# RWKV scan: chunks of 64 tokens for 32, each 64×64 inverse joined from two 32-row blocks

## What the stage computes

```python
def wkv_scan(r, logw, k, v, a, b, s0):
    def step(s, inp):
        r_t, lw_t, k_t, v_t, a_t, b_t = inp
        sa = jnp.einsum('dbhij,dbhj->dbhi', s, a_t)
        s = s * jnp.exp(lw_t)[..., None, :] + sa[..., None] * b_t[..., None, :] + v_t[..., None] * k_t[..., None, :]
        return s, jnp.einsum('dbhij,dbhj->dbhi', s, r_t)
    s_fin, y = lax.scan(step, s0, (tm(r), tm(logw), tm(k), tm(v), tm(a), tm(b)))

def rwkv_readout(y, prep, r_k, lnx_g, lnx_b, w_out):
    yf = y[0] + jnp.flip(y[1], 1)
    mean = jnp.mean(yf, axis=-1, keepdims=True)
    var = jnp.mean(jnp.square(yf - mean), axis=-1, keepdims=True)
    yn = ((yf - mean) * lax.rsqrt(var + GN_EPS)).reshape(B, T, D).astype(gate.dtype) * lnx_g + lnx_b
    bonus = jnp.sum(r[None] * k_dir * r_k, axis=(0, -1))[..., None] * v
    o = (yn + bonus.reshape(B, T, D)) * jax.nn.silu(gate)
    return o @ w_out
```

## Time and profile before

| | |
|---|---|
| median of 3 runs | 2717.05 us (2715.08 to 2720.73) |
| profiled run | 2720.06 us, span 2718.4 us |
| busy share of the span: PE, PEld, DVE, ACT, POOL | 83%, 64%, 36%, 19%, 2% |
| mean granted clock of TensorE, whole span | 0.858 of full speed |
| scan stage, 1640 to 2353 us | 713 us, of them PE busy 573.3, DVE 307.2, ACT 264.7; clock 0.67 |

### The profile page before, as it was taken

The page is one execution under the profiler, slowest core; times in us unless marked ns, Lnnn a source line. Parts: engine busy times, 40 slices in busy tenths (PEclk is TensorE's granted clock), DMA queues, the critical chain, the costliest instruction groups (busy, mean ns, idle before and its releaser), DMA issues. The chain is left out here.

```text
span 2718.4 us, 39159 instructions
## 1 busy us (share of the span) xinstructions
PE 2245.3 (83%) x16630; PEld 1735.0 (64%) x16630; DVE 984.4 (36%) x2209; ACT 518.1 (19%) x920; POOL 58.2 (2%) x85
## 2 busy tenths in 40 slices
PE   1999955798999886899859993688888889779797
PEld 0888854687888775788624442466666777536445
DVE  3224346411440372675161003544544441120253
ACT  1011022401000101100110003444444333010142
POOL 0000000000000300000000000000000000000000
PEclk9999977898999898899979995776667776689889
DMA  7465410424874321775303203111101111312100
GB/s 289 173 230 228 171 64 8 86 93 165 336 280 155 124 78 37 281 302 217 138 16 109 92 31 125 38 39 38 35 15 39 29 25 41 124 66 93 52 10 16
DMA packets 103014, 305.14 MB, mean 112 GB/s; under 512 B 71352, under 2 KB 79800, under 8 KB 85184
## 3 DMA queue, kind: packets, MB, share of 16 engines
q1 hardware_dynamic: 94384, 225.11, 24.3%
q0 software_dynamic: 8464, 77.60, 7.3%
HBM read 286.88 MB, written 15.80 MB: 111 GB/s over the span
## 5 line engine op out<-in xcount | busy, mean ns | idle before, releaser
L263 PE MATMUL bank<-h,ring 128*128 128x256 f32 x2944 | 646.7, 383 | 22.8 <-DVEq L967 15.3
L263 PEld LDWEIGHTS bank<-h,ring 128*128 128x128 f32 x2944 | 566.3, 193 | 104.0 <-DVEq L967 16.0
L263 PE MATMUL bank<-mixed,ring 128*128 128x512 f32 x384 | 165.0, 592 | 1.3 <-DVE mixed L1249 1.3
L877 PE MATMUL bank<-ffn_hidden,ring 128*128 128x256 f32 x704 | 152.4, 379 | 3.3 <-PEq L903 3.3
L877 PEld LDWEIGHTS bank<-ffn_hidden,ring 128*128 128x128 f32 x704 | 133.6, 190 | 22.2 <-issue 4.1
L263 PEld LDWEIGHTS bank<-mixed,ring 128*128 128x128 f32 x384 | 72.9, 190 | 93.5 <-issue 91.4
L156 DVE CUSTOM_DVE_ANT_0 next_w<-next_w,next_vec,par 128x1024 f32<-128x1024 f32 x96 | 120.1, 1279 | 11.4 <-DMA next_w<-in_mod_stream 11.4
L1987 DVE TENSOR_TENSOR rw_u<-bank,rw_lam 128x128 f32<-128x128 f32 x120 | 35.0, 291 | 236.1 <-PE bank L1660 233.1
L889 DVE SCALAR_TENSOR_TENSOR x<-bank,mod,x 128x256 f32<-128x256 f32 x24 | 10.0, 477 | 231.6 <-PE bank L877 231.6
L1668 PE MATMUL bank<-rw_gr,rw_u 64*64 64x32 f32 x960 | 80.3, 252 | 13.0 <-DVE rw_u L1987 12.9
L1581 PE MATMUL bank<-rw_xa,ring 64*64 64x64 f32 x1024 | 30.5, 305 | 72.2 <-DVE rw_xa L1920 72.2
(11 more groups left out here) (387 smaller groups left out, 3415.1 us busy)
## 6 DMA issues: line engine op xcount, KB each, us to landing
ring<-in_stream SPq DMA_DIRECT2D x89, 2048.0 KB, 8.0
next_w<-in_mod_stream POOLq DMA_DIRECT2D x24, 2048.0 KB, 9.9
ctx<-in_mod_rest POOLq DMA_DIRECT2D x16, 1024.0 KB, 7.3
rwkv_projections<-proj_out POOLq DMA_DIRECT2D x8, 1024.0 KB, 6.7
y<-bias_table SPq DMA_DIRECT2D x48, 128.0 KB, 4.9
rw_rkv<-rwkv_projections SPq DMA_DIRECT2D x8, 768.0 KB, 4.2
rw_at<-rw_at_kept SPq DMA_DIRECT2D x16, 256.0 KB, 3.9
rwkv_o<-rwkv_projections POOLq DMA_DIRECT2D x1, 2048.0 KB, 16.0
```

Source lines behind the costliest of these rows:

```text
L263: mm = pe.matmul(out, ring_tile(k, n, kt, i * P), rhs[kt], start=start and kt == kts[0], stop=stop and kt == kts[-1])
L877: mm = pe.matmul(k.psum[grp * 4 + i][:, 0:T], ring_tile(k, n, kt, i * P), rhs[part * KT + kt], start=(part == 0 and kt == 0), stop=(part = ...
```

## The change

It works in chunks of 64 tokens: 8 chunks, chain items 0 to 8, seven state updates. The inverse stays at 32×32 blocks (`SUB`), 64 of them per n as before: each chunk's 64×64 matrix has two diagonal blocks that VectorE inverts, and the block between them comes from two new products on TensorE, `left` and `join`, each with a ScalarE copy behind it (four items for each n, 16 matmuls of 32×32 with 32 columns each). For `left`, the first diagonal block's inverse is needed transposed too: VectorE copies all inverses in turned order (L1995), SyncE stores part of that in four more DMAs (L1537, 64-byte runs) and loads it in two more (L1544). SyncE also waits for `left` of the n before (`left_up`) ahead of the loads.

Keys of a chunk lie on rows 0 to 63 and second factors on rows 64 to 127. So akv and pq use one 64×64 tile, `inner` and `read_inner` tiles of 128 rows by 64 columns, `carried` and `read_state` 64×64; grams fill 64×128 and come in four halves for each n, masked in pieces of 256 elements. The gate is loaded for each n. The two numbers that place an item list in the period change for five lists.

```diff
-LCH = 32
+LCH = 64
+SUB = 32
 NCK = 512 // LCH
...
 def scan_solve(n):
 
+    out = [("left", n, 0), ("atok", n, 0, 0), ("left", n, 1), ("atok", n, 0, 1), ("join", n, 0)]
+    for d in range(2):
+        out += [("akv", n, d, e) for e in range(2)]
+        out += [("atok", n, 1, half) for half in range(2)] + [("join", n, 1)] if d == 0 else []
+        out += [("pq", n, d, e, half) for half in range(2) for e in range(2)]
+        out += [("gr", n, d)]
+    return out
...
-                            (0, 0.7, has(i + 1, scan_solve(i + 1))),
-                            (0, 0.3, has(i + 2, scan_grams(i + 2))),
+                            (0, 0.75, has(i + 1, scan_solve(i + 1))),
+                            (0.1, 0.42, has(i + 2, scan_grams(i + 2))),
                             (0, 0.3, has(i - 1, scan_read(i - 1))),
...
-                            (0.45, 1, has(i + 2, [("inv", i + 2, s) for s in range(1, LCH)])),
-                            (0.42, 1, has(i + 3, scan_ready(i + 3))))
+                            (0.55, 1, has(i + 2, [("inv", i + 2, s) for s in range(1, SUB)])),
+                            (0.48, 0.9, has(i + 3, scan_ready(i + 3))))
...
                 for q in range(2):
                     sp.dma_start(own_rows(mt_dram, n, q), Xb[rows64(q)]).then_inc(x_out, 16)
-                sp.wait_ge(x_out, 32 * (n + 1))
+                    for d in range(2):
+                        at = 64 * q + 32 * d
+                        sp.dma_start(first_turned(n, d, q), turned_back(ATb)[at:at + 16]).then_inc(x_out, 16)
+                sp.wait_ge(x_out, 96 * (n + 1))
+                if n:
+                    sp.wait_ge(left_up, 2 * n)
                 for d in range(2):
-                    for h in range(2):
-                        sp.dma_start(BG[n % 3][d][brows(h), :, :, 96:128].rearrange("p c e t -> p (c e) t"),
-                                     blocks(mt_dram, n, d, h)).then_inc(mt_in, 16)
+                    for i in range(2):
+                        sp.dma_start(on_chip(n, d, i), blocks(mt_dram, n, d, i)).then_inc(mt_in, 16)
+                    sp.dma_start(TM[d][sub(0)], bass.AP(m1_dram, (n % 2) * 32 * 1024 + d * 16 * 1024,
+                                                        [[SUB, SUB], [1024, 16], [1, SUB]])).then_inc(mt_in, 16)
...
+            def left(n, d):
+                u = 2 * n + d
+                pe.wait_ge(mt_in, 96 * (n + 1))
+                pe.wait_ge(gram_down, 4 * u + 4)
+                out = take("left", n, d)
+                for c in range(NCK):
+                    for e in range(2):
+                        j = 2 * c + e
+                        mm = pe.matmul(out[sub(1), SUB * j:SUB * j + SUB], AA[n % 2][d][sub(0), c, e, SUB:LCH],
+                                       TM[d][sub(0), j, :], start=True, stop=True)
+                mm.then_inc(left_up, 1)
+                free(left_down, u + 1, "left", n, d)
+
+            def join(n, d):
+                u = 2 * n + d
+                pe.wait_ge(left_down, u + 1)
+                out = take("join", n, d)
+                for c in range(NCK):
+                    for e in range(2):
+                        j = 2 * c + e
+                        mm = pe.matmul(out[sub(0), SUB * j:SUB * j + SUB], TM[d][sub(1), j, :],
+                                       AA[n % 2][d][sub(1), c, e, SUB:LCH], start=True, stop=True)
...
             def inner(n, c):
-
-                h, c2 = c % 2, c // 2
                 for d in range(2):
                     for e in range(2):
-                        mm = pe.matmul(k.psum[h][rows64(e), 64 * d:64 * d + 64], BG[n % 3][d][rows64(h), c2, e, 0:64],
-                                       VQ[n % 2][d][rows64(h), c2, e, :], start=(d == 0), stop=(c == 0), skip_group_check=True)
+                        mm = pe.matmul(k.psum[c % 2][rows64(e), 64 * d:64 * d + 64], BG[n % 3][d][:, c, e, 0:64],
+                                       VQ[n % 2][d][:, c, e, :], start=(d == 0), stop=(c == 0), skip_group_check=True)
                 return mm
...
                     for q in range(2):
                         one = xf[rows64(q), q:q + 34 * 15 + 1:34]
-                        ins = v.tensor_scalar(one, one, 1.0, None, ALU.add)
-                    ins.then_inc(inv_done, 1)
+                        s(v.tensor_scalar(one, one, 1.0, None, ALU.add))
+                    v.tensor_copy(turned_back(ATb), Xb.rearrange("p j t -> p t j")).then_inc(inv_done, 1)
```

More of the change, by code:

```diff
@@ L1530, in _ @@
         def _(pool):
[L1531 to L1532 removed]
+            for n in range(KT):
+                if n:
+                    pool.wait_ge(o_done, n)
+                pool.dma_start(sg, kept[n, :, 3, :]).then_inc(gate_in, 16)
+            pool.wait_ge(gate_in, 16 * KT)
         @block.tensor
@@ L1605, in solved @@
                 u = 2 * n + d
-                pe.wait_ge(mt_in, 64 * (n + 1))
+                pe.wait_ge(join_down, u + 1)
                 pe.wait_ge(akv_down, 2 * u + e + 1)
                 out = take("pq", n, d, e, half)
-                at = slice(4 * half, 4 * half + 4)
-                for h in range(2):
-                    pe.matmul(out[krows(h), :].rearrange("p (c v) -> p c v", c=4)[:, :, 64:128],
-                              ident[krows(h), krows(h)], VQ[n % 2][d][krows(h), at, e, :], start=True, stop=True)
@@ L1613, in solved @@
                 for j in range(4):
-                    c2 = 4 * half + j
-                    for h in range(2):
-                        x, y = VQ[n % 2][d][brows(h), c2, e, :], KP[d][brows(h), c2, e, :]
-                        both = bass.AP(x.tensor, x.offset, [list(x.ap[0]), [y.offset - x.offset, 2], [1, 64]])
-                        mm = pe.matmul(out[brows(h), j * P:(j + 1) * P], BG[n % 3][d][brows(h), c2, e, 96:128], both,
-                                       start=True, stop=True)
+                    c = 4 * half + j
@@ L1620, in solved, with steps_made @@
+                    x, y = VQ[n % 2][d][BR, c, e, :], KP[d][BR, c, e, :]
+                    both = bass.AP(x.tensor, x.offset, [list(x.ap[0]), [y.offset - x.offset, 2], [1, 64]])
+                    mm = pe.matmul(out[BR, j * P:(j + 1) * P], AA[n % 2][d][BR, c, e, :], both, start=True, stop=True)
                 mm.then_inc(pq_up, 1)
                 free(pq_down, 4 * u + 2 * half + e + 1, "pq", n, d, e, half)
-            def steps_made(n, d, half):
+            def steps_made(n, d):
                 u = 2 * n + d
-                pe.wait_ge(pq_down, 4 * u + 2 * half + 2)
@@ L1724, in _ @@
                 elif kind == "gram":
-                    grams(n, item[2])
+                    grams(n, *item[2:])
+                elif kind == "left":
+                    left(n, item[2])
+                elif kind == "join":
+                    join(n, item[2])
                 elif kind == "btok":
```

226 lines of the change are left out of this document (122 added, 104 removed).

## The result

The changed kernel takes 2844.4 us (median of 4 runs, 2843.1 to 2862.1); the kernel before took 2716.3 beside it. The ratio is 1.047, 95% interval 1.044 to 1.051: slower, as forecast, inside the range of 2728 to 2870, but by 128 us where the forecast had 68.

A forecast was written before the change was run, and what follows sets the result against it. The prediction took TensorE's stream to bound the scan stage; −2.7 work, +16.6 boundary, +4.0 elements and −8.2 vanished waits made +9.7 us a period, +68 over seven boundaries: 2785 us, whole range 2728 to 2870.

The forecast's parts named there:

- (f): Period boundary: `left` waits for the inverse through VectorE's tail and SyncE's trip, +16.6 us a period.
- rival B: Clock falls further behind the boundary's longer wait: +10 us a period, 2865 us; chance 0.15.
- (a): TensorE's chain: full steps fall from 13 to 5 a period, −12.1 us; longer reads charged nothing.
- (d): Grams on TensorE: two products at a time instead of four, time doubles, +3.1 us a period.
- (c): New `left` and `join` on TensorE: four items of 16 matmuls on one 32×32 tile each, +6.0 us a period.
- (g): Second direction's elements on VectorE stand behind the last three readout operations: +4.0 us a period.
- (h): TensorE's earlier waits for next-pair elements and state updates vanish: −8.2 us a period.
- At the ends … cancel: Ends of the scan stage: filling, +5 us, and the last period, −5 us, cancel.
- (e): Step matrices on TensorE: 2048 columns per half for 2304, −1.5 us a period.
- C: Weight loads show on single-tile `left`, `join`, `akv`, `pq`: +18.5 us a period, 2933 us; chance 0.04.
- D: Faster: fewer, fuller items let TensorE stay at 2.4 GHz behind the boundary, 2681 us; chance 0.10.
- E: Boundary covered: VectorE's tail fits beside TensorE's, the trip ends in time, waits stay: 2695 us; chance 0.03.

The follow-up runs named there:

- the two-order run: Changed kernel with `left` and `join` behind the first direction's key products and the second direction's elements ahead of the readout's last three operations: 2739.4 us.
- the first order: Changed kernel with only `left` and `join` moved behind the first direction's transposes and key products: 2744.5 us.

## Why the prediction was right, and by how much it was not

**The direction and its cause were right.** (f), the wait of `left` for the inverse, was named as the largest term with VectorE's tail and SyncE's trip, and both measure within half a microsecond of it. Moving the wait away gives back 100 of 128 us. That the time still lies inside the range owes something to luck: its width stood for TensorE's work, the trip and rival B, and more than half of the miss lies outside the four steady periods, where the sum had the two ends cancel.

**(f) was undersized by 3.8 us a period: 20.4 for 16.6.** The failing step is "9.0 low or 4.6 high, mean 7.3" for TensorE's own tail. A mean price fits a whole period, not one short piece of it. In the changed kernel the tail ran at the full clock (1.00 from 2172.5 to 2176.7) and took 4.2 us, a little under the high end that the working itself had; with that end taken, (f) would have come to 19.3. The trace of before could not settle the level: the boundary there was at the low one.

**(a) to (d): the work.** Charged were 18 shape changes at 0.10 us, +1.8; measured are 0.15 at each of four per step at 1.2 GHz, and a step of 2.50 and 1.52 us for 1.85 and 0.95. "I charge nothing" for the longer reads was nearly right, 0.12. At the period's mean clock of 0.68 (64% low) five steps cost 5 × 2.15 = 10.7 us; forecast were 5 × 1.51 + 1.8 = 9.3. `left` and `join` (c) are busy 6.9 us for 6.0, and the grams (d) rose by 3.9 for 3.1. TensorE's busy time fell by 1.8 us instead of 2.7 in that period, so this part of the sum held, within 1 us.

**(g) was 5.9 us for 4.0**, in two waits (3.1 and 2.8) that the forecast had as one. What it costs in time is not shown: the run that moved the elements gained mostly by the clock, and the two-order run shows no gain beyond the first order's. **(h)** had 8.2 us vanish; all 10.7 did.

**"At the ends … cancel" was the largest miss.** Over the spans of the two profiled executions the change is +123.7 us. The four steady intervals that the sum was made for gave 52.4 (forecast 39). The filling and the first two intervals gave 52.9 (forecast 24). By the sum's own terms the first interval had to be dearer: with no full chain steps to save, (a) is nothing there and (c), (d) and (e) stand alone, +7.6 for the −2.7 that was charged. Besides, the wait for the inverse is longer (25.9 us), and the mean clock is lower, 0.60 for 0.76 in the first interval and 0.63 for 0.74 in the second, which is rival B in one part of the stage. How the 52.9 divide among the three was not tested. The last interval and the end gave 12.1 (forecast 5). The remaining 6.3 lie outside the stage, 3.3 ahead of it and 3.0 behind, in code that the change does not touch; that was not followed up.

**The rivals.** B did not come in the steady part (mean clocks of the four periods 0.64, 0.72, 0.68 and 0.68 for 0.69), only in the first two intervals. C: `left`, `join`, `akv` and `pq` on a single tile pass their records 58, 119 and 238 ns apart at 1.2 GHz for 32, 64 and 128 columns (2197.12 to 2198.96 above; 16 records of L1650 from 1775.34 to 1777.24 and 8 of L1664 from 2240.45 to 2242.35 in the same trace). The spacing follows the columns alone, also from L1650 to L1664, whose weights are alike 64×64, so the weight loads lie beside the matmuls. The Trainium skill, "TensorE: Matmul & The Clock Gate", on packing small matmuls, has a load overlap only where the row group differs; these rows do not agree. D did not come: the clock did not rise. Its premise, that fuller work raises the clock, has support from the runs that add whole-array matmuls; that the change makes the work fuller is not shown. E's condition, a covered boundary, was met by the other order alone, and the time was then 2744.5 and 2739.4 us, not E's 2695.

With the order mended the change still gains nothing. In the last steady period of that run TensorE is busy 73.0 us at a mean clock of 0.67, for 71.1 at 0.69 before: once shape changes and the two products of the join are paid, its work is no less.

## What to carry to other kernels

When a change puts a new first item at the head of each round, ask what that item waits for and where the producer ends; the place of `left` in the table of items was worth 100 us here. Where the clock has two levels, price a short piece of work at both and keep both ends, and cost the first and last rounds by themselves. Where TensorE runs at half clock although it is busy, fewer columns or rows can come out slower, as two runs here did in their periods: look at the granted clock of an experiment before reading its time as the price of what was taken out.

## What was not expected of the hardware

- Taking work out slowed TensorE: half the read columns, 2844 to 2882 us in one run, with the mean clock of the four steady periods at 0.57 to 0.64 for 0.64 to 0.72. Adding 15.5 us of 128×128 matmuls to a period of the kernel before left two of its four steady periods at 81.5 us (81.9) and made the other two 86.2, the clock going from 0.69 to 0.83 and up to 0.88.
- With TensorE busy 36.8 of 40.9 us the clock stayed at 1.2 GHz, in work mostly on 32×32, 64-row and 128×64 tiles; filling the idle time ahead of it did not prevent the fall. Yet 10 us of much the same tiles, without a gap, ran at 2.4 GHz later in the period. Whole-array matmuls raise the mean grant; what decides it at one place these runs leave open.
- A change between 64×64 and 128×64 tiles costs 0.15 us at 1.2 GHz. The Trainium skill, "TensorEngine Tiling (Array Packing)", section on tiling modes, says that a mode switch requires a drain. The trace fits that: within one shape the records of neighbouring groups interleave, across a change in these rows they do not.
